# Gate and up weights as the stationary operand in four feed-forwards of a float32 block kernel

## The reference, cut to what matters

```python
def swiglu(x, w_gate, w_up, w_down):
    return (jax.nn.silu(x @ w_gate) * (x @ w_up)) @ w_down
```

## Time and profile before

| | us |
|---|---|
| median of three runs | 2607.17 |
| the profiled execution: its time | 2606.88 |
| its span, first to last instruction | 2605.0 |
| first feed-forward, one step of 512 columns | 33.57 |
| second and third, one step with a window | 34.46 |

### The profile page before, as it was taken

One profiled execution on the slowest core, in us unless ns is written; L12 is line 12 of the kernel. 1 busy time (PEld: TensorE's weight loads), 2 busy tenths in 40 slices (PEclk: granted clock), 3 DMA queues, 4 the chain that ended last, 5 costly groups with the idle time before them and its releaser, 6 DMA issues.

```text
span 2605.0 us, 35035 instructions
## 1 busy us (share of the span) xinstructions
PE 2578.4 (99%) x12506; PEld 2139.0 (82%) x12506; DVE 2002.6 (77%) x2322; ACT 1685.5 (65%) x2239; POOL 166.2 (6%) x207
## 2 busy tenths in 40 slices
PE   9999999999999999999999999999999999999998
PEld 7888888888888878888678888788888888888886
DVE  5557667778767765564678876899999999999998
ACT  5446664454467875453564444788888888888887
POOL 2000000000000001005210000400000000000020
PEclk9999999999999999999999999999999999999999
DMA  9555237768754349543149885799999999999997
GB/s 323 188 176 194 65 128 262 249 229 314 243 178 154 115 151 343 195 150 129 49 168 334 311 270 157 268 394 390 381 383 372 395 367 390 375 385 376 383 381 289
DMA packets 286860, 690.58 MB, mean 265 GB/s; under 512 B 12756, under 2 KB 25456, under 8 KB 286752
## 3 DMA queue, kind: packets, MB, share of 16 engines
q1 hardware_dynamic: 267648, 619.51, 66.6%
q0 software_dynamic: 19104, 69.62, 7.9%
HBM read 673.34 MB, written 15.75 MB: 265 GB/s over the span
## 4 chain that ended last, share of the span: by engine, by line
PE 93%; ACT 3%; DVE 2%; DMA 1%; issue 1%; POOL 0%; ACTq 0%; DVEq 0%; SPq 0%
PE ps L2679 27%; PE ps L2684 27%; PE ps L2680 27%; PE ps L2759 2%; PE ps L2958 2%; PE ps L3027 1%; ACT w_hi L939 1%; DMA w_raw<-in_moe_w 1%; PE ps L3425 0%; DVE w_lo L1740 0%; PE ps L2720 0%; ACT hp L1378 0%; PE ps L3491 0%; PE ps L3269 0%; PE ps L3519 0%
## 5 line engine op out<-in xcount | busy, mean ns | idle before, releaser
L1740 DVE TENSOR_TENSOR w_lo<-w_raw,w_hi 128x1024 fp32r<-128x1024 f32 x1149 | 1379.1, 1225 | 395.2 <-ACT w_hi L939 370.4
L939 ACT ACTIVATE w_hi<-w_raw 128x1024 fp32r<-128x1024 f32 x1152 | 1201.0, 1057 | 707.4 <-PE ps L2684 697.5
L2679 PE MATMUL ps<-w_hi,act_hi 128*128 128x512 f32 (+2 forms) x3328 | 1287.7, 389 | 4.8 <-ACT scr L1332 1.7
L2680 PE MATMUL ps<-w_hi,act_lo 128*128 128x512 f32 (+2 forms) x3328 | 1269.7, 384 | 0.0
L2684 PE MATMUL ps<-w_lo,act_hi 128*128 128x512 f32 (+2 forms) x3328 | 928.4, 384 | 1.4 <-DVE w_lo L1740 1.3
L2679 PEld LDWEIGHTS ps<-w_hi,act_hi 128*128 128x128 f32 x3328 | 625.7, 188 | 128.4 <-ACT w_hi L939 3.9
L2680 PEld LDWEIGHTS ps<-w_hi,act_lo 128*128 128x128 f32 x3328 | 626.1, 188 | 118.7 <-issue 1.4
L2684 PEld LDWEIGHTS ps<-w_lo,act_hi 128*128 128x128 f32 x3328 | 613.3, 188 | 128.3 <-DVE w_lo L1740 4.3
L1727 DVE SCALAR_TENSOR_TENSOR scr<-scr,small 128x1024 f32<-128x1024 f32 x98 | 125.3, 1279 | 5.5 <-DMA scr<-in_ada_w 5.5
L1872 DVE TENSOR_TENSOR act_lo<-ps,act_hi 128x512 fp32r<-128x512 f32 (+1 forms) x87 | 74.1, 852 | 40.2 <-ACT act_hi L1113 40.2
L1113 ACT ACTIVATE act_hi<-ps 128x512 fp32r<-128x512 f32 (+1 forms) x87 | 62.7, 720 | 62.2 <-PE ps L2958 62.2
(11 more groups left out here) (540 smaller groups left out, 1542.3 us busy)
## 6 DMA issues: line engine op xcount, KB each, us to landing
w_raw<-in_moe_w SPq DMA_DIRECT2D x338, 1024.0 KB, 9.3
scr<-in_ada_w POOLq DMA_DIRECT2D x48, 1024.0 KB, 7.0
w_raw<-in_ffn_w_up SPq DMA_DIRECT2D x44, 1024.0 KB, 5.3
w_raw<-in_ffn_w_down SPq DMA_DIRECT2D x44, 1024.0 KB, 4.9
w_raw<-in_ffn_w_gate SPq DMA_DIRECT2D x43, 1024.0 KB, 5.2
w_raw<-in_ff_w SPq DMA_DIRECT2D x42, 1024.0 KB, 6.8
w_raw<-in_odd_w_in SPq DMA_DIRECT2D x19, 1024.0 KB, 5.1
w_raw<-in_even_w_in SPq DMA_DIRECT2D x13, 1024.0 KB, 5.3
```

The costliest lines, as they stand in the source:

```text
L939: act.activation(w_hi[:, split_at(g), 0:c * width], w_raw[:, s % RING, o:o + c * width], ACT.Copy).then_inc(hi_done, 1)
L1740: dve.tensor_tensor(w_lo[:, split_at(g), 0:c * width], w_raw[:, s % RING, o:o + c * width], w_hi[:, split_at(g), 0:c * width].bitcast(F32) ...
L2679: pe.matmul(out_ap, act_hi[:, chunk, cols], whi, start=start, stop=False)
L2680: pe.matmul(out_ap, act_lo[:, chunk, cols], whi, start=False, stop=False)
```

## The change

The first step of 512 columns stays as it was, with its transposes. The other 2304 hidden columns are done in nine steps of 256. There a block of 128 x 128 of the gate or up weights is stationary, and the activations move: the high and the low part lie side by side (`acts`), so one product with 512 moving columns is high by high and low by high, and a second one, 256 wide, takes `w_lo` by the high activations. The result has hidden columns on its partitions, so it needs no transpose, but it lies in two halves of a bank that have to be added. The norm factor is now one for each moving column; a row of them (`rn_row`) is made once by a small product. The up part is left without it, and `boundary` puts it in later. Each granule of these steps is one bank: 128 hidden columns by 1024.

Planner (order of the granules) and tables:

```diff
+        def plan_crossed(wg, wu, wd, ff):
+            m_last = crossed_steps(ff)
+            plan_up(wg, 0, BANK)
+            plan_up(wu, 0, BANK)
+            for m in range(1, m_last + 1):
+                f = BANK + PAIR * (m - 1)
+                plan_up(wg, f, PAIR, False)
+                plan_up(wu, f, PAIR, False)
+                if m == 1:
+                    plan_down(wd, 0, BANK)
+                elif m < m_last - 1:
+                    plan_down(wd, f - PAIR, PAIR)
+            plan_down(wd, ff - 3 * PAIR, 3 * PAIR)
...
-        SUMS_FIRST = {3: 0, 4: 6, 5: 1}
-        SUMS_SECOND = {1: 7, 2: 2, 3: 3, 4: 4, 5: 5}
+        SUMS_FIRST = {6: 0, 8: 6, 9: 1}
+        SUMS_SECOND = {2: 7, 4: 2, 6: 3, 8: 4, 9: 5}
-        CTX_WINDOWS = {2: 0, 3: 1}
+        CTX_WINDOWS = {4: 0, 6: 1}
```

ACT, one step:

```diff
+                for m in range(1, last + 1):
...
+                    hi(crossed_downs(ff, m))
+                    act.wait_ge(gran_used, base + crossed_at(ff, m) + 2)
+                    act.activation(gate_sum, ps[:, 4:6, TOKENS:BANK], ACT.Copy).then_inc(silu_done, 1)
+                    act.wait_ge(hid_done, n(hid_done))
+                    act.activation(gate_silu, gate_sum, ACT.Silu).then_inc(silu_done, 1)
+                    hi(2)
+                    act.wait_ge(gran_used, base + crossed_at(ff, m) + 4)
+                    act.activation(crossed_hid, ps[:, 6:8, TOKENS:BANK], ACT.Copy).then_inc(silu_done, 1)
+                    crossed_high(m)
+                    hi(2)
```

DVE, one step (`scaled` is true in all four):

```diff
+                    lo(crossed_downs(ff, m))
+                    dve.wait_ge(silu_done, n(silu_done))
+                        link(dve.tensor_tensor(gate_sum, ps[:, 4:6, 0:TOKENS], gate_sum, ALU.add))
+                        dve.tensor_tensor(gate_sum, gate_sum, bc_mid(rn_row, 2), ALU.mult).then_inc(hid_done, 1)
...
+                    lo(2)
+                    dve.wait_ge(silu_done, n(silu_done, 2))
+                    link(dve.tensor_tensor(crossed_hid, ps[:, 6:8, 0:TOKENS], crossed_hid, ALU.add))
+                    dve.tensor_tensor(crossed_hid, crossed_hid, gate_silu, ALU.mult).then_inc(hid_done, 1)
+                    dve.wait_ge(hid_done, n(hid_done, 2))
+                    if windows and m in windows:
+                        context_columns(windows[m]) if sums is None else column_sums(windows[m])
...
+                    lo(1)
+                    crossed_low(m)
+                    lo(1)
```

PE, a granule and one step:

```diff
+                def crossed_up(bank):
+                    g = gp[0]
+                    pe.wait_ge(hi_done, g + 1)
+                    for k in range(DC):
+                        pe.matmul(ps[:, bank, :], w_hi[:, split_at(g), k * P:(k + 1) * P], acts[:, :, k, :], start=k == 0, stop=False)
+                    pe.wait_ge(lo_done, g + 1)
+                    for k in range(DC):
+                        ins = pe.matmul(ps[:, bank, 0:TOKENS], w_lo[:, split_at(g), k * P:(k + 1) * P], act_hi[:, k, :],
+                                        start=False, stop=k == DC - 1)
...
+                for m in range(1, last + 1):
+                    pe.wait_ge(silu_done, n(silu_done, 3) - 1 if m > 1 else n(silu_done))
+                    if windows and m - 1 in windows:
+                        pe.wait_ge(mod_red, n(mod_red))
+                    crossed_up(4)
+                    if m == 1:
...
+                    crossed_up(5)
...
+                        pe.wait_ge(hid_done, n(hid_done, 2))
+                    crossed_up(6)
+                    crossed_up(7)
+                    if windows and m in windows:
+                        turn_context(windows[m], 2) if sums is None else turn_sums(sums, windows[m], 2)
...
+                    elif m != last - 1:
+                        pe.wait_ge(hlo_done, n(hlo_done))
+                        of = min(m - 1, last - 2)
+                        down([crossed_slot(of), crossed_slot(of) + 1])
+                pe.wait_ge(silu_done, n(silu_done, 3) - 1)
+                if closing:
+                    closing()
...
+                pe.wait_ge(hlo_done, n(hlo_done, 2))
+                return [crossed_slot(m) + k for m in (last - 1, last) for k in range(2)]
```

More of the change, by code:

```diff
@@ L938, in hi @@
                         act.wait_ge(gran_used, n.gran(split_freed(g) + 1))
-                    act.activation(w_hi[:, split_at(g), 0:c * width], w_raw[:, s % RING, o:o + c * width],
-                                   ACT.Copy).then_inc(hi_done, 1)
+                    act.activation(split_part(w_hi, g, c, width), raw_part(g, c, width, o), ACT.Copy).then_inc(hi_done, 1)
                 gp[0] += k
@@ L1007, in _, with boundary @@
             tail_end = [0]
-            def boundary(col, late, ahead_of=1):
+            def boundary(col, late, ahead_of=1, crossed=False):
                 tail_end[0] = gp[0]
@@ L1912, in gated, with crossed, crossed_low @@
                     beside(len(s))
+            def crossed(ff, scaled=False, beside=None, sums=None, windows=None):
+                last = crossed_steps(ff)
+                def crossed_low(m):
+                    dve.wait_ge(hhi_done, n(hhi_done))
+                    at = crossed_slot(m)
+                    dve.tensor_tensor(act_lo[:, at:at + 2, :], crossed_hid, act_hi[:, at:at + 2, :].bitcast(F32),
+                                      ALU.subtract).then_inc(hlo_done, 1)
+                if scaled:
+                    for tb in range(TB):
+                        dve.tensor_scalar(rn_diag[:, tb * P:(tb + 1) * P], ident, rn[:, tb:tb + 1], None, ALU.mult)
+                    dve.tensor_scalar(rn_half, rn[:], 0.5, None, ALU.mult)
+                lo(4)
+                layer[0] = sums
+                lo_ahead(2)
+                dve.wait_ge(silu_done, n(silu_done))
+                dve.wait_ge(gran_used, gp[0])
+                dve.tensor_tensor(hp[:].rearrange("p (b n) -> p b n", b=TB), sg[:].rearrange("p (b n) -> p b n", b=TB),
+                                  ps[:, 6:8, :], ALU.mult).then_inc(hid_done, 1)
+                n(hid_done)
+                lo(2)
+                if scaled:
+                    dve.wait_ge(mod_tp, n(mod_tp))
+                    dve.tensor_copy(rn_row, ps[:, 3, 0:TOKENS]).then_inc(mod_red, 1)
+                    dve.wait_ge(mod_red, n(mod_red))
+                dve.wait_ge(hhi_done, n(hhi_done))
+                dve.tensor_tensor(act_lo[:, 8:12, :], banks(6, 2).rearrange("p (c n) -> p c n", c=4),
+                                  act_hi[:, 8:12, :].bitcast(F32), ALU.subtract).then_inc(hlo_done, 1)
+                lo(2)
+                for m in range(1, last + 1):
+                    if beside and m % 2 == 0:
+                        beside(m // 2)
+                    lo(crossed_downs(ff, m))
+                    dve.wait_ge(silu_done, n(silu_done))
+                    if scaled:
+                        link(dve.tensor_tensor(gate_sum, ps[:, 4:6, 0:TOKENS], gate_sum, ALU.add))
+                        dve.tensor_tensor(gate_sum, gate_sum, bc_mid(rn_row, 2), ALU.mult).then_inc(hid_done, 1)
+                    else:
+                        dve.tensor_tensor(gate_sum, ps[:, 4:6, 0:TOKENS], gate_sum, ALU.add).then_inc(hid_done, 1)
+                    lo(2)
+                    dve.wait_ge(silu_done, n(silu_done, 2))
[4 more added lines that the diff above has]
+                        context_columns(windows[m]) if sums is None else column_sums(windows[m])
+                        if sums == 1 and windows[m] == MOD_G1 // 8:
+                            next_gate()
+                    if m == last:
+                        if sums == 1:
+                            mod_columns(1)
+                        layer[0] = None
+                    lo(1)
+                    crossed_low(m)
+                    lo(1)
+                if beside:
+                    beside(len(steps(ff)))
@@ L3415, in odd, with turn_sums @@
                 return [o_slot(c) for c in range(12, 16)], [(og_lo, 7), (og_lo, 8)]
-            def turn_sums(l, nb):
+            def turn_sums(l, nb, silu=1):
                 context = nb >= 6
@@ L3421, in turn_sums @@
                 pe.wait_ge(ada_sum, 64 * l + ready)
-                pe.wait_ge(silu_done, n.last(silu_done) + 1)
+                pe.wait_ge(silu_done, n.last(silu_done) + silu)
                 src = m_sumc[:, DM * (nb - 6):DM * (nb - 5)] if context else m_sum[:, DM * nb:DM * (nb + 1)]
@@ L3426, in turn_sums, with turn_context @@
                 ins.then_inc(mod_tp, 1)
-            def turn_context(w):
-                pe.wait_ge(silu_done, n.last(silu_done) + 1)
+            def turn_context(w, silu=1):
+                pe.wait_ge(silu_done, n.last(silu_done) + silu)
                 if w == 0:
@@ L3689, in _ @@
             lead_first(4)
-            tail(gated(FF1, scaled=True, closing=more_rows), 0)
+            tail(crossed(FF1, scaled=True, closing=more_rows), 0)
             lead(4)
@@ L3694, in _ @@
             lead(4)
-            tail(gated(FF1, scaled=True, sums=0, windows=SUMS_FIRST), 0)
```

(5 more changed lines are left out.)

139 lines of the change are left out of this document (109 added, 30 removed).

## The result

The kernel after takes 2656.05 us (median of four runs, 2650.67 to 2657.51), the one before beside it 2607.35 (four runs, 2606.31 to 2608.64). The ratio is 1.0183, with an interval of 1.0167 to 1.0199: 48.7 us slower, where 32.3 were forecast. The forecast's range was 2610 to 2656, so the measured time lies at its very end. The profiled execution took 2657.51, with a span of 2655.7, and 2655.7 - 2605.0 = 50.7 us are to be found in the trace.

The account below looks back on a forecast made before the run. PE, busy 99% of the span, was taken as the bound. PE's work of -7.6 us plus 39.9 us of new waits gave +32.3 on 2606.88, so 2639 us, with a range of 2610 to 2656.

Parts of the forecast that it names:

- PE's own work: Products, transposes, rn_row product and width changes on PE: -1.90 us per feed-forward, -7.6 over four.
- item 1: End of each feed-forward: PE waits for the last step's low part, 2.3 + 3.1 + 3.1 + 2.6 = 11.1 us.
- item 2: Step 8's window, second and third feed-forward: no down products cover the reduction; mean wait 4.6, twice, 9.2 us.
- item 3: Other windows with down products (step 6; steps 2, 4, 6): chain outlasts its cover, 2.1, 2.1, 0.9, 2.1 = 7.2 us.
- item 4: Silu at the windows with down products: turn_sums waits for the same step's silu, 4.0, 2.2, 1.8, 0.6 = 8.6 us.
- item 5: Splits that come late in steps 3 to 5 of the second feed-forward: five times 0.4 to 0.9 = 3.8 us.
- clock at its lower level: Long PE waits of 4 to 5 us drop the clock to half: 5 us at three places, left in the range.
- The other small operations: Diagonals of rn and a scale on a square: said to stand where DVE is half idle; no wait counted.
- the prediction's own sign: Forecast is wrong if, among other signs, the first feed-forward changes by more than 3 us either way.
- loop that tips over: Rival: splits or adds 10 to 20% dearer, every step of second and third waits; 2655 to 2670 us, chance 0.12.
- All is covered: Rival: DVE and ACT idle time hides everything, only PE's work changes; 2599 us, chance 0.10.
- only the chains without accumulates: Rival: accumulates slip into DVE's gaps, late splits, silu and other-window waits vanish, rest shrinks to 12; 2611.5 us, chance 0.12.

Follow-up runs that it names:

- e1: Kernel after, with the first feed-forward's matrix of ones for rn_row made by a memset at the start instead of taken from the late constants; 2643.2 us.
- e2: Kernel after, with the first table's 64 accumulates cut to 16 columns in place of 1024, sums left incomplete; 2632.8 us.
- e3: Kernel after, with DVE doing crossed_low ahead of the two splits in step 9, not between them; 2646.8 us.
- e6: Kernel after, with DVE's multiply of the summed gate by rn_row left out in all nine steps of the four feed-forwards; 2640.6 us.
- e5: Kernel after, with 22 products of zeros, 512 wide in plain float32, ahead of the first feed-forward's wait for the late constants; 2664.8 us.
- e7: Kernel after with the edits of e1 and e3 (2636.4 us), plus zero products ahead of three long PE waits in second and third feed-forward; 2634.7 us.
- e4: Kernel after, with the sums' window of step 8 moved to step 7, and that of step 6 to step 5 in the second feed-forward; 2649.1 us.
- e8: Kernel after, with accumulates moved from behind the down splits to the other splits, at 15 of 16 of them; 2651.5 us.

## Why the forecast was right in kind and low in size

By the steps of the prediction, in us over the four feed-forwards:

| step | forecast | measured |
|---|---|---|
| PE's own work | -7.6 | about -6.9, by its rows |
| item 1, ends | 11.1 | 2.34 + 3.05 + 0.90 + 2.71 = 9.0 |
| item 2, window in step 8 | 9.2 | 4.69 + 2.63 = 7.3 |
| item 3, other windows | 7.2 | 0.18 + 1.78 + 0.61 + 1.80 = 4.4 |
| item 4, silu | 8.6 | 3.90 + 1.93 + 1.70 + 0.17 = 7.7 |
| item 5, late splits | 3.8 | 1.6 |
| wait for the constants | not seen | 9.5 |
| clock at its lower level | 0 (5 in a rival) | about 10.6 |
| PE starting again behind some 18 waits, 0.2 each | not seen | about 3.5 |
| attention to router, and rest | 0 | 2.1 + 0.5 |
| sum | 32.3 | about 49 of 50.7 |

**PE's work: right but for one small term.** Eight wide and eight narrow products take 2.79, where 2.773 + 0.02 was forecast. The product for `rn_row` I had at 0.27. In after's second feed-forward:

```profile
410.20 0.60 PE L3196 MATMUL ps<-xt,cst 128*128 128x256 f32 x2
410.45 2.18 PE L3173 MATMUL ps<-acts,w_hi 128*128 128x512 f32 x8
```

The first narrow product behind these starts at 412.46, 2.26 us from the start of the small one, where eight wide products alone take 1.82: it costs 0.44. One product in plain float32 stands in the trace as two records (x2), and the sixteen of the earlier trace rows are eight products; I had divided by the records. That is 0.7 us over four. (The transposes' figures add up to 4.13, not the 4.17 of the sum.) The first feed-forward of e1, where the clock never falls, fits the sum: PE is busy 206.58 us there and 208.37 in before, -1.8. The other price weighed there, an estimate of 0.216 and 0.109 per product (the Trainium skill, "TensorE: Matmul & The Clock Gate", section "Back-to-back issue gap"), would have made the granule 2.60; the trace, with 2.77 to 2.79, decides for the rows.

**The chains: right, up to the backlog and the floors.** Where DVE's backlog was as in my table, a wait could be laid out to 0.1 us from durations and order: the second's step 8 was 4.69 for 4.6, its silu 3.90 for 4.0, the ends 2.34 for 2.3, 3.05 for 3.1 and 2.71 for 2.6. e2, e3 and e6 show the chains' members one by one: without accumulates 17.8 us of 25.0 go, the split ahead of `crossed_low` was 6.6 at the ends, the multiply 0.7 at three of the four. The backlog was too large in my table: I let the 64 accumulates run on to the end. In the third feed-forward they are done by step 8, so its step 8 waits 2.63 and its end 0.90, where I had 4.6 and 3.1. These are also under the floors "of 4.2 twice, without any backlog" and "of 1.9 four times", and e2 has the same without accumulates (2.6 twice; 1.06 and 0.91). Item 2 had an ACT split and a DVE split, 2.20 together, between PE's last product and the add; without a backlog they are done by then, and ACT's copy of 0.60 stands in their place. At the ends of the second and third PE's transposes of the sums, 0.8, cover a part. That, item 3 and the late splits make items 1 to 5 30.0 instead of 39.9.

**The step that failed: "The other small operations (the diagonals of `rn`, a scale on a square) stand where DVE is half idle."** I priced the product for `rn_row` as PE's work, 0.27, and did not ask what it waits for. The product stands 147 us ahead of the first place that needed the late constants before. So "The first and fourth feed-forward should change by under 1 us each" is false: +12.1 and +2.9, and 11.4 of the first are shown by e1 to be this wait and what it does to the clock. By the prediction's own sign ("or if the first changes by more than 3 us either way") it was wrong there. That the time still came out at the end of the range is partly luck: the range was made wide for dearer splits and a loop that tips over, which did not come, and not for this wait. My terms gave +0.4 and +0.7, the end waits less the work. In the fourth the end wait came as forecast (2.71), and most of what is more is a fall of the clock from 1186.8 on, 3.4 us long, which costs 1.5.

**The clock: priced as a rival, and too low.** I had up to 5 us at three places. ("the one fall of the clock" in before is not the only one: a second, from 2600.6 to its end, stands behind PE's work and costs nothing.) The rows have PE busy 196.03 us in the second where it was 189.84: +6.2 for work that should be 1.7 less. Its clock was low for 13.7 us in three falls, from 514.4, 555.4 and 579.3 on; less the idle time in them, half of it is lost: 6.0. The third lost 1.7 (its mean is 0.99), the fourth 1.5 and the first 1.4. In the first e5 shows the cause, PE's standing still for 9.5 us. The Trainium skill, same page, section "HAM oscillation — how this bites in real kernels", says that long idle gaps of PE put the clock to half; the 9.5 us wait agrees (0.61 in 37.8 to 51.0). Falls behind short waits it doesn't cover: e7 has three with no wait over 2.0 us. All experiments that took idle time away (e2, e3, e4, e6) got back more than that time, above all in the second feed-forward. In the profiles of all changed versions each fall within these four feed-forwards begins during a wait of PE or at most 1.4 us behind the end of one, and the shortest such wait is 1.80 us (e7, e6). But other waits pass without a fall, 3.05 us long in e8 (ended at 578.05) and 2.34 in after (198.78). So waits and falls go together, and which wait calls one is open.

**The rivals.** "All is covered" and "only the chains without accumulates" are out by PE's 25 us of idle time. Of the loop that tips over, only the clock came true: DVE stands at 162.26 of 209.52, 77%, not at its limit; PE did not wait in every step, and strided splits cost what plain ones do (1221 ns mean in the second feed-forward, 1229 over all of before). "DVE should be at 85 to 90%" is false for the stage, 77%, and for a step of 16.61 without waits too, where DVE is busy 13.18 us, 79%.

The number 2639 was thus low by 17: -10 for the items, +0.7 for `rn_row`, +9.5 for the constants, +10.6 for the clock, +3.5 for restarts, +2 for a stretch that varies by itself. Waits too high and costs not seen cancel in part.

## What to carry to other kernels

A form that gives the bounding engine less work isn't faster when it adds members to a chain between engines and takes away what stood between its ends: 7 us less work brought 30 us of waits here, and those can be laid out beforehand from durations and the order on each engine, in which the last item of a queue counts as much as the chain. For each new operation, however small, write down every semaphore that it waits for and when that was last satisfied in the old trace; the costliest single wait here (9.5 us) was ahead of a product of under 0.5 us. And where such waits break up PE's stream, allow for the clock: about 11 us came on top of 30 and the 9.5.

## What the runs showed of the hardware

- The clock can fall behind a short wait, and with PE at work again. In e7 it fell at 510.4, 1.2 us behind the end of a wait of 1.80 us; PE is busy for all of 4.00 us from 510 to 514, at a granted clock of 0.57. In e8 a wait of 3.05 us passed without a fall. Two profiles of the kernel before differ by 1.3 us in one stretch, at clocks of 1.00 and 0.99.
- 22 products of 128x512 in plain float32, issued one behind the other, took 18.9 us, 0.86 each, against 0.227 for the reduced form. The trace has two records for each, 44 in all.
- A wait costs PE some 0.2 us more than its idle time: the first feed-forward's, second's and third's busy times exceed work and clock by that much per wait. No run was made for it, but rows show where it can lie: behind the wait that ends at 198.78 the next product starts 0.34 us later and not 0.227, and the last product ahead of a wait counts as busy for its full 0.39.
